# Layer B's value product: its second pass loads 64 stationary columns and alternates with the next head's transposes, and filling steps stand ahead of it

## The reference, cut to what matters

```
def swa_mixer(q, k, v, q_norm, k_norm, sink):
...
        s = jnp.einsum('bqkgd,bjkd->bkgqj', q_blk, k_blk).astype(jnp.float32) * scale
        s = jnp.where(valid, s - slopes * dist, NEG)
        sk = jnp.broadcast_to(sink_l, s.shape[:-1] + (1,))
        p = jax.nn.softmax(jnp.concatenate([s, sk], axis=-1), axis=-1)[..., :-1]
        return jnp.einsum('bkgqj,bjkd->bqkgd', p.astype(v_blk.dtype), v_blk)
```

## Time and profile before

| | us |
|---|---|
| median of 3 runs | 1342.72 (1342.25 to 1344.69) |
| profiled execution, its own time | 1341.16 |
| span of its trace, first to last instruction | 1339.0 |
| PE busy | 1334.1, in 6968 products and as many loads |
| DVE, ACT, POOL busy | 894.9, 675.7, 387.7 |

### The profile page before, as it was taken

The page is one execution under the profiler, slowest core; times in us unless marked ns, Lnnn a source line. Parts: engine busy times, 40 slices in busy tenths (PEclk is TensorE's granted clock), DMA queues, the critical chain, the costliest instruction groups (busy, mean ns, idle before and its releaser), DMA issues.

```text
span 1339.0 us, 20089 instructions
## 1 busy us (share of the span) xinstructions
PE 1334.1 (100%) x6968; PEld 1155.8 (86%) x6968; DVE 894.9 (67%) x1819; ACT 675.7 (50%) x1532; POOL 387.7 (29%) x495
## 2 busy tenths in 40 slices
PE   9999999999999999999999999999999999999999
PEld 7889988888888888898888898888888888898997
DVE  6886688878796746887792424767766634147873
ACT  6554466655564645777651413545444323147761
POOL 0421252330011323655302213422300122236552
PEclk9999999999999999999999999999999999999999
DMA  8968744333779897633775455332144553563405
GB/s 307 323 232 286 255 151 173 129 139 134 255 231 397 292 376 266 228 109 103 283 250 191 166 165 179 103 114 98 45 149 156 197 177 112 192 227 107 147 28 188
DMA packets 107635, 256.55 MB, mean 192 GB/s; under 512 B 11152, under 2 KB 42768, under 8 KB 107536
## 3 DMA queue, kind: packets, MB, share of 16 engines
q1 hardware_dynamic: 102064, 247.58, 52.8%
q10 hardware_dynamic: 5472, 7.69, 1.9%
HBM read 167.15 MB, written 88.08 MB: 191 GB/s over the span
## 4 chain that ended last, share of the span: by engine, by line
PE 99%; DVE 0%; issue 0%
PE bank L2065 27%; PE bank L2067 27%; PE bank L2066 27%; PE bank L2110 9%; PE bank L2426 3%; PE bank L2071 3%; PE bank L2072 2%; PE bank L2143 0%; PE bank L2158 0%; DVE xs L1852 0%; PE bank L2171 0%; DVE actT L1501 0%; DVE ones L1500 0%; DVE mhalf L1499 0%
## 5 line engine op out<-in xcount | busy, mean ns | idle before, releaser
L2065 PE MATMUL bank<-actT,w_split 128*128 128x512 f32 x544 | 215.5, 396 | 0.0
L2067 PE MATMUL bank<-actT,w_split 128*128 128x512 f32 x544 | 212.3, 390 | 0.0
L1937 POOL TENSOR_TENSOR prob<-prob,rinv 128x256 f32<-128x256 f32 x192 | 130.8, 713 | 253.8 <-DVE rinv L1447 253.7
L1274 DVE TENSOR_TENSOR w_split<-w_raw,w_split 128x512 fp32r<-128x512 f32 (+2 forms) x199 | 139.3, 715 | 75.4 <-ACT w_split L852 72.1
L852 ACT ACTIVATE w_split<-w_raw 128x512 fp32r<-128x512 f32 (+2 forms) x199 | 120.1, 616 | 119.3 <-PE bank L2067 45.1
L2065 PE MATMUL bank<-w_split,actT 128*128 128x512 f32 (+3 forms) x448 | 159.0, 355 | 0.0
L2066 PE MATMUL bank<-w_split,actT 128*128 128x512 f32 (+3 forms) x448 | 158.9, 355 | 0.0
L2067 PE MATMUL bank<-w_split,actT 128*128 128x512 f32 (+3 forms) x448 | 158.9, 355 | 0.0
L2066 PE MATMUL bank<-actT,w_split 128*128 128x512 f32 x384 | 149.8, 390 | 0.0
L871 ACT ACTIVATE sq<-bank 128x384 f32<-128x384 f32 (+3 forms) x124 | 59.6, 489 | 145.1 <-PE bank L2067 135.6
L1298 DVE TENSOR_REDUCE ss<-sq 128x2 f32<-128x384 f32 (+5 forms) x116 | 62.8, 554 | 99.5 <-ACT sq L871 98.8
(11 more groups left out here) (197 smaller groups left out, 3066.4 us busy)
## 6 DMA issues: line engine op xcount, KB each, us to landing
w_split<-kept_w SPq DMA_DIRECT2D x125, 512.0 KB, 3.3
kept_w<-w_split SPq DMA_DIRECT2D x107, 512.0 KB, 5.4
kept_w<-part_split SPq DMA_DIRECT2D x33, 512.0 KB, 5.4
w_raw<-in_w_mem SPq DMA_DIRECT2D x64, 256.0 KB, 3.1
part_split<-kept_w SPq DMA_DIRECT2D x29, 512.0 KB, 4.0
w_raw<-in_w_b SPq DMA_DIRECT2D x51, 256.0 KB, 4.8
w_raw<-in_w_out SPq DMA_DIRECT2D x35, 256.0 KB, 4.4
w_raw<-in_w_a SPq DMA_DIRECT2D x32, 256.0 KB, 4.4
```

The costliest lines, as they stand in the source:

```text
L1274: dve.tensor_tensor(halves(n)[1], w_raw[:, RAW_AT[n] % RAW, 0:width], halves(n)[0].bitcast(fp32), ALU.subtract).then_inc(w_lo_dve, 1)
L1937: pool.tensor_tensor(t, t, rinv[:, par, i:i + 1].to_broadcast(list(t.shape)), ALU.mult).then_inc(p_pool, 1)
L2065: nc.tensor.matmul(out, lhs[0], rhs[0], start=start, stop=False, skip_group_check=skip)
L2067: return nc.tensor.matmul(out, lhs[1], rhs[0], start=False, stop=stop, skip_group_check=skip)
```

## The change

Five things change. (1) In `b_o` the pass with the low half of the probabilities (`a=1`) loads only the 64 high value columns; the product of low values and low probabilities is no longer summed into rows 64 to 127. All four key blocks now take the first pass, and then all four the second. (2) `b_pt` becomes a generator, and one transpose of the next head stands ahead of each of the four second-pass products; the other six follow them. (3) The filling steps of the first place stand ahead of the scores, and those of the second place ahead of the value product. (4) On ACT, `o_low` stands behind the exponentials of head `h+2`, on DVE `b_sum` behind `b_p(h + 2)`. (5) Tables: `WINDOW_FILL` (sums now 17 and 23), `SPLIT_AT` (pair 1 after head 5 instead of 4, pair 4 after head 10 instead of 11), and in `BANK_USE` the last two figures of `part` (1.6, 0.5 to 2.6, 0.9) and `bqT` (3.2, 0.8 to 3.8, 1.0) and the third of `bQ` (5.0 to 5.3), `bkT` (1.8 to 2.8), `bS` (3.0 to 2.3), `bPT` (1.5 to 2.5) and `bO` (2.3 to 2.0). `FILL` is written otherwise but keeps its values.

```
-WINDOW_FILL = [(1, 2), (1, 2), (2, 1), (1, 1), (1, 2), (1, 2), (0, 2), (1, 1), (1, 2), (1, 1), (1, 2), (1, 1), (2, 2), (0, 1), (2, 0), (2, 0)]
+WINDOW_FILL = [(0, 2), (2, 2), (2, 1), (2, 2), (0, 1), (1, 2), (0, 2), (1, 1), (1, 2), (0, 2), (1, 2), (1, 1), (1, 2), (1, 1), (2, 0), (2, 0)]
...
-SPLIT_AT = {3: (0,), 4: (1,), 6: (2,), 8: (3,), 11: (4,), 13: (5,), 15: (6,), 16: (7,)}
+SPLIT_AT = {3: (0,), 5: (1,), 6: (2,), 8: (3,), 10: (4,), 13: (5,), 15: (6,), 16: (7,)}
...
-                            b_low(h)
                             fill(min(1, WINDOW_FILL[h][1]))
                             chunk_end()
                             if h + 2 < HB:
                                 b_exp(h + 2)
                             fill(max(0, WINDOW_FILL[h][1] - 1))
+                            b_low(h)
                             if h + 1 < HB:
                                 b_pt(h + 1)
...
-                            b_sum(h)
                             fill(WINDOW_FILL[h][1])
                             if h + 2 < HB:
                                 b_p(h + 2)
+                            b_sum(h)
...
+                        def b_o(h, a, turned=None):
                             use = ("bO", L, h)
-                            pe.wait_ge(*vacant(use))
-                            c = h // (HB // KVB)
-                            order = [k for blocks in SHARED for k in blocks]
+                            if a == 0:
+                                pe.wait_ge(*vacant(use))
+                            c = h // (HB // KVB) * P
+                            rows = P if a == 0 else HD
                             for k in order:
                                 lo_q, hi_q = window(k)
                                 s, col = SHARED_AT[k]
-                                pe.wait_ge(*read(("bPT", L, h, s)))
-
-                                for a in range(2):
-                                    ins = nc.tensor.matmul(
-                                        bank(use)[:, lo_q * P:(hi_q + 1) * P], v0[:, 0, k, c * P:(c + 1) * P],
-                                        windowT[h % 2][:, a, SHARED_FROM[s] + col:SHARED_FROM[s] + col + span(k)],
-                                        start=k == order[0] and a == 0, stop=k == order[-1] and a == 1, skip_group_check=True)
-                            ins.then_inc(full(use)[0], 1)
+                                if a == 0:
+                                    pe.wait_ge(*read(("bPT", L, h, s)))
+                                elif turned is not None:
+                                    next(turned)
+                                ins = nc.tensor.matmul(
+                                    bank(use)[0:rows, lo_q * P:(hi_q + 1) * P], v0[:, 0, k, c:c + rows],
+                                    windowT[h % 2][:, a, SHARED_FROM[s] + col:SHARED_FROM[s] + col + span(k)],
+                                    start=k == order[0] and a == 0, stop=k == order[-1] and a == 1, skip_group_check=True)
+                            if a == 1:
+                                ins.then_inc(full(use)[0], 1)
...
                         for h in range(HB):
+                            fill(WINDOW_FILL[h][0])
                             if h + 2 < HB:
                                 b_s(h + 2)
-                            fill(WINDOW_FILL[h][0])
                             if h % 2 == 0 and h + 4 < HB:
                                 b_q(h // 2 + 2)
                             if h + 3 == HB // 2:
                                 b_k(1)
-                            b_o(h)
                             fill(WINDOW_FILL[h][1])
-                            if h + 1 < HB:
-                                b_pt(h + 1)
+                            b_o(h, 0)
+                            turned = b_pt(h + 1) if h + 1 < HB else None
+                            b_o(h, 1, turned)
+                            for _ in turned or ():
+                                pass
```

More of the change, by code:

```diff
@@ L341, in plan @@
             for h in range(HB):
+                fill(stream, WINDOW_FILL[h][0])
                 if h + 2 < HB:
                     take([("bS", L, h + 2, s) for s in range(len(SHARED))])
-                fill(stream, WINDOW_FILL[h][0])
                 if h % 2 == 0 and h + 4 < HB:
@@ L348, in plan @@
                     take([("bkT", L, 1)])
-                take([("bO", L, h)])
                 if h == B_BARE:
@@ L355, in plan @@
                 fill(stream, WINDOW_FILL[h][1])
+                take([("bO", L, h)])
                 if h + 1 < HB:
@@ L2412, in b_pt @@
                                 pe.wait_ge(p_pool, pool_count(L, NT * (MH + h) + i + 1))
-                                transposes(use, parts)
-                        def b_o(h):
+                                for c, src in enumerate(parts):
+                                    ins = nc.tensor.transpose(bank(use)[:, c * P:(c + 1) * P], src, ident[:])
+                                    if c == len(parts) - 1:
+                                        ins.then_inc(full(use)[0], 1)
+                                    yield
+                        order = [k for blocks in SHARED for k in blocks]
+                        def b_o(h, a, turned=None):
                             use = ("bO", L, h)
-                            pe.wait_ge(*vacant(use))
-                            c = h // (HB // KVB)
-                            order = [k for blocks in SHARED for k in blocks]
+                            if a == 0:
+                                pe.wait_ge(*vacant(use))
+                            c = h // (HB // KVB) * P
+                            rows = P if a == 0 else HD
                             for k in order:
@@ L2440, in _ @@
                         fill(FILL["b_second"])
-                        b_pt(0)
+                        for _ in b_pt(0):
+                            pass
                         for h in range(HB):
+                            fill(WINDOW_FILL[h][0])
                             if h + 2 < HB:
                                 b_s(h + 2)
-                            fill(WINDOW_FILL[h][0])
                             if h % 2 == 0 and h + 4 < HB:
```

16 lines of the change are left out of this document (3 added, 13 removed).

## The result

The changed kernel takes 1344.36 us (median of 21 runs, 1343.09 to 1345.35); the kernel before took 1341.94 in 21 runs on the same chips. The ratio is 1.0017, 95% interval 1.0011 to 1.0023: slower by 2.4 us.

What follows compares the result with a forecast made beforehand. PE's own row of products, busy for all of the span, was taken as the bound. Terms: 0.5 less 0.2 less 0.4 is -0.1 us, no change; forecast median 1342.6 us, 1341 to 1344 in this case, whole range 1335 to 1358.

Steps and rivals of the forecast that it cites:

- The two waits of head 3: PE's loads waiting for DVE in layer B; more filling steps ahead of the value product should remove both, saving 0.4 us.
- wait of a transpose for POOL: Sign against the step on probabilities wanted earlier: head 14 had 3.2 us slack, 1.95 used up; no cost was taken.
- case (a): On PE, a transpose streams at half speed, holding 0.109 itself; alternating then gains only 0.002 a pair, 0.2 us.
- The sign that I named for this: Distance from a transpose inside the value product to the 64-column product behind: 0.11 as forecast, 0.055 under rival 1.
- Rival 1: On PE, a transpose waits for its load; 120 pairs save 6.5 us, giving a median of 1336.3; chance 28%.
- rival 2: On PE, switching stationary shape costs time: 0.118 a pair, 14.2 us, giving 1356.8; chance 29%.
- My 0.5 for more steps from product to transpose: On PE, 120 more steps from a product to a transpose, at 0.004 each, cost 0.5 us.
- A new place to wait: `o_low` and `o_pair` now delay copies before PE's next value product; ready at 3.14, product starts at 3.5; no cost taken.
- margin of 0.7: Slack in us between the copies behind `o_pair` being ready and the next value product needing the last tile.
- Tables ... Nothing: SP's list keeps its order and pair 1's later split comes before its sums are read; no cost taken.
- Rival 3: The margin of 0.7 is too small; 0.2 us in each of 30 heads costs 6 us, 1348.6; chance 5%.

Runs made afterwards that it cites:

- e2: The changed kernel, but the second pass loads 128 stationary columns again: 1344.84 us, 1.0019 of the kernel before.
- e3: The kernel before, with only the second pass narrowed to 64 stationary columns, order and tables as before: 1342.79 us, 1.0004 of the kernel before.
- e10: The kernel of e9 with the last two figures of `part` at 2.0 and 0.5: 1342.24 us, 1.0005 of the kernel before.
- e9: The changed kernel, but in heads 3, 5 and 8 all transposes stand behind the value product: 1341.35 us, 1.0000 of the kernel before.
- e1: The changed kernel, but at heads 4, 6 and 9 one second-place filling step stands ahead of the scores again: 1346.75 us, 1.0035 of the kernel before.
- e5: The changed kernel with filling steps respread so heads 3 to 13 have at least one at both places: 1344.40 us, 1.0019 of the kernel before.
- e8: The changed kernel with only the figures of `part` as before (1.6, 0.5): 1344.44 us, 1.0022 of the kernel before.

## Why the forecast was wrong

**Right.** PE's own row sets the time. The two waits of head 3 went (0.4), and the list has no wait of a transpose for POOL. A transpose of 128 columns holds PE for 0.109 by itself and not for a load, case (a): in a pair its own load has long begun when it starts, and the product behind it needs only half a load, and yet the period of a pair is 0.29 and 0.23, the sum of 0.109 and the long product's 0.17 or 0.12. The loads show the transpose's share:

```profile
570.64 0.14 PEld L2423 LDWEIGHTS bank<-probT,v 128*64 128x64 f32 x1
570.76 0.14 PEld L2403 LDWEIGHTS bank<-ident,prob 128*128 128x128 f32 x1
570.93 0.14 PEld L2423 LDWEIGHTS bank<-probT,v 128*64 128x64 f32 x1
```

The load behind the narrow one begins 0.12 after the transpose's start at 570.64, and the next at the next transpose's start. The sign that I named for this, the distance of starts from a transpose to the product behind it, was a bad one: it reads 0.03 in any case, as at 570.01 in the earlier trace rows. Rival 1 (a gain of 0.055 a pair) is ruled out by e2, rival 2 (a price of the shape) by e3 and by the distances above. The Trainium skill's rule on loads that I weighed ("TensorE: Matmul & The Clock Gate", "LDWEIGHTS (loading the stationary operand)") gives 53 ns less for 64 columns as an estimate; the records agree with 52, but a load that hides is worth nothing, so the gain worked out from it did not come. What the Trainium skill says of a mode change ("TensorEngine Tiling (Array Packing)", "Key Properties") does not show here: if a tile of 128 by 64 is another mode, 256 changes into and out of it cost less than 1.7 us in e3. My 0.5 for more steps from product to transpose was too much: a step onto a transpose from 384 columns takes the 0.17 it should. By the ends of the records the pairs of the profile after take 0.286 and 0.227 on average, and the two parts of each took the same in the kernel before to within half a nanosecond, under 0.1 us for all 120.

**The step that failed** is "A new place to wait", together with "Tables ... Nothing". I wrote that behind `o_low` and `o_pair` "waits the next value product on PE", worked out that `o_pair` ends 1.54 after the start of the last 64-column product (0.28 + 0.04 + 0.62 + 0.60), and found a margin of 0.7 for the copies behind it. That margin, for `windowT`, holds: the list has no wait of the value product. But `o_pair` does a second thing: as last reader it frees the value product's bank, and I did not ask the planner who gets it. At three rounds of each layer B it is the third score bank, with no filling step between. By my own figures it was wanted 0.12 (that product) + 0.65 (six transposes) + 0.69 (four score products) = 1.46 after the same start and free at 1.54: 0.08 late, where the text shows a margin of 0.7. That alone would have named the six places. The profile after has the bank 0.16 late: from the product's end (571.47 + 0.36) to `o_pair`'s end (573.18) it is 1.35, where I had 1.26, since I took for `o_pair` the 0.60 to DVE's next start, and its record is 0.67 in the earlier trace rows and 0.68 here. What makes 0.32 of it, the start behind the release and the load that no longer hides, had no term either. For "Tables" I had weighed SP's list and when pairs are split, not at `BANK_USE`, whose figures say which bank a use follows.

**The term that was missing** is +2.3, and layer A's +0.4 is another of the same step: a table's figures for `part`, changed for layer B's sake, are used in layer A as well. Rival 3 had the right chain and the wrong waiter, and asked for 0.1 us in each of 30 heads where six heads paid 0.3 to 0.4.

What is left open: the 0.1 us at the query transposes of rounds 4 and 6 fits the end of DVE's first difference (573.22 + 0.53), which is the last reader of the bank that the planner gives these transposes, but no run took it alone. e10 stands 0.9 above e9, where its two waits less layer A's four make 0.5; the spread of the runs doesn't tell these apart.

## What to carry to other kernels

When an instruction is moved later, list everything that it releases, not only the data it makes: a last reader frees a buffer, and a planner may have given that buffer to work that stands near. Ask the planner, for each moved step, which use follows it on the same bank and how much work lies between; a place where a table puts no filling work between is where to look for the wait first. And in a plan this tight a repair at one place (e1, e5, e8, e10) tends to open a wait at another: take away the cause at the places where it costs (e9), and leave the rest alone.

## What was not expected of the hardware

A stationary tile of 64 instead of 128 columns shortens the load's record from 188 to 136 ns and moves no product: the distances behind it are 0.17 and 0.12 as before. PE went between 128- and 64-column tiles 256 times in e3 at no measurable cost, under 1.7 us in all.
